# Hybrid decoder step: DeltaNet's z blocks 10 to 21 moved in halves into the attention's loop over pairs, with the convolution in pieces beside them

## The chip, the cores and the metric

One core of one Trainium2 chip runs the whole step in one launch. The metric is the device time in microseconds, the median of the runs shown. Engines: TensorE (PE) multiplies, its weight loads are shown apart (PEld), VectorE (DVE), ScalarE (ACT) and GpSimd (POOL) work elementwise, SyncE (SP) issues most of the DMAs. The engines run their own streams and meet at semaphores.

## What is computed

Two layers over N = 520 columns of width 1024: 512 prompt tokens and 8 single-token samples (T = 512, B = 8, HALF = 260). Per layer:

```python
x = x + 1/2 * SwiGLU_1(RMSNorm(x))
h = RMSNorm(x); z = h @ w_in
A: sparse attention (compressed / selected / window branches)
B: gated DeltaNet (short causal conv on q/k/v, delta rule in chunks)
C: HGRN2
x = x + merge(A, B, C) @ w_out
x = x + 1/2 * SwiGLU_2(RMSNorm(x))

def causal_conv(x_new, buf, w):        # before the delta rule
    xx = concatenate([buf, x_new], axis=1)
    return sum(xx[:, j:j + T] * w[j] for j in range(4))
```

With 512 tokens and 64-token blocks all blocks are selected, so the selected and the window branch are both plain causal attention over 512 rows with their own K and V.

## The kernel before

**Layout.** Everything stands transposed: 128 features on the partitions, 520 columns in the free dimension. z is made in 42 blocks of 128 columns of w_in (zi): 0 to 9 are the attention's q, k and v, 10 to 21 DeltaNet's q, k and v (four each), 22 to 25 its output gate, 26 to 41 HGRN2's; a small tile (gates, decays) comes after block 9. A product in f32 accuracy is made of three f16 products, w_hi by h_hi, w_hi by h_lo and w_lo by h_hi, so a block is 8 depths by 3 products by 2 halves of 260 columns, 48 matmuls (`products`, L2018 to L2030, called by `z_block`).

**Weights.** Each weight tile is fetched by SP (L2007, 512 KB) into one of two raw buffers, ScalarE makes w_hi (`split_hi`, L2012), GpSimd makes w_lo (`split_lo`, L2016); the ring has four tiles. SP may fetch tile n when tile n - 2 is split. SP goes through the tiles in order and has other DMAs in between: after z tile 16 the attention's new K and V are written back, after tile 17 DeltaNet's states are loaded (`D.load`, L816 and L817, behind `wait_left`: the attention is done), and after tile 43, the last of z, DeltaNet's outputs are written (`D.write_back`, L819 to L826, behind the step sa7). The first tiles of the merge (in_w_mg) are fetched only after that.

**The attention's loop over pairs** (`A.tensor`, `scalar`, `vector`, `pool`). For each of 4 query blocks t of 128 tokens there are 8 pairs (branch b, head column c), each of both KV groups g; 32 pairs i in all, and the scores of pair i have width w = 128 (t + 1). Per pair PE makes two score products in f32 (L349, K = 64), VectorE adds the distances and takes the minimum (L607), ScalarE exponentiates (L473), VectorE inverts the sums (L612), GpSimd scales (L513), PE transposes (L360), ScalarE and VectorE copy the two halves (L485, L623), and after four pairs PE makes the value products (L386). PE's stream runs scores(i), turn(i - 3), and values of the group before. The scores of a pair use banks 0 to 3 by turns, the transposes 4 and 5, the outputs 6 and 7. Each layer also has compressed scores turned (L368) and their values (L376).

**DeltaNet.** `for zi in range(10, 26)`: z_block, then `D.during_z`, which puts column sums of squares (`sums`, L894 and L895) after blocks 18 and 22 and the decay sums (gcl) after 24. ScalarE copies each block to cx (L1172 to L1174, or silu to dz, L1176), and for groups of four takes silu of the convolved rows (L1182) and squares (L1185). VectorE waits for a group of four blocks and then convolves, four taps by four rows of 512 columns (L1291, L1293). Then `D.tensor` runs the chunked delta rule, some 120 us in which PE waits for the chain of the other engines.

**Blocks 26 to 41** run with DeltaNet's end in between (`D.during_next`): after 26 small sums, after 27 and 28 the products with the 32 sample states (16 each, L1105), after 29 and 30 the norm sums (L1143, L1148), after 32 to 35 a spread (L1114), after 36 to 39 two outer products each (L1121). `vector_states` adds each to the states and gives sa0 to sa7 (L1496, L1500). HGRN2's own stage starts with sa7. A block zi waits until block zi - 2 has been copied, and ScalarE's copy of a block stands behind its split for the block before.

## Time and profile before

| | us |
|---|---|
| runs of the kernel before | 3437.97, 3439.61, 3445.85 (median 3439.61) |
| profiled execution, its own time | 3443.68 |
| its span, first to last instruction | 3441.9 |
| PE busy | 3154.1 (92%) |
| VectorE, ScalarE, GpSimd busy | 1078.4, 1082.3, 1129.9 |
| mean granted clock of TensorE | 0.926 of full speed |

The profiled execution took 1.8 us more than its span and lies 4.1 us above the median of the runs. PE's busy time contains waits inside its pipeline, so it is an upper bound of its work. The trace gives start and duration of each instruction, what ended the idle time before it, and for any stretch the busy time of each engine and the clock granted to TensorE (1.00 is 2.4 GHz, 0.50 is 1.2 GHz).

### The profile page before, as it was taken

Reading aid. Unit: us, or ns where it says so; the run is one execution under the profiler, and the core shown is the slowest. Engines: PE = TensorE matmul, PEld = TensorE weight load, DVE = VectorE, ACT = ScalarE, POOL = GpSimd, SP = SyncE. Lnnn points to the kernel's source line nnn. Section 1 sums busy time; section 2 is a strip of 40 time slices with the busy share of each in tenths; the row PEclk is TensorE's granted clock in tenths of the full one; section 3 lists DMA queues with packets and bytes.
Section 4 is the critical chain, followed back from the end, with each engine's and each line's share of the span. In section 5 each row is a group of like instructions: output and inputs, shape, how many; then the busy total and the mean of one; then the engine's idle time right before and its main releaser. Section 6 shows DMA issues by size and latency. Waiting matters only on the chain.

```text
span 3441.9 us, 69990 instructions
## 1 busy us (share of the span) xinstructions
PE 3154.1 (92%) x29292; PEld 2717.5 (79%) x29292; DVE 1078.4 (31%) x1981; ACT 1082.3 (31%) x1846; POOL 1129.9 (33%) x664
## 2 busy tenths in 40 slices
PE   6999898897888998999989998978978889989999
PEld 5888796387777887888878887864877788878887
DVE  3221202454244335221232212033542444352212
ACT  3332222432222323333233323224412223233322
POOL 3443320333121343443434443113331213334434
PEclk9999995998897999999999999959988979989999
DMA  4343320030021332332323433200200303323333
GB/s 142 114 149 89 115 88 1 1 106 20 26 96 40 93 120 80 98 98 87 104 90 117 138 95 119 67 1 33 87 8 28 125 27 93 120 74 98 98 92 116
DMA packets 87637, 283.27 MB, mean 82 GB/s; under 512 B 13330, under 2 KB 26514, under 8 KB 84882
## 3 DMA queue, kind: packets, MB, share of 16 engines
q1 hardware_dynamic: 87298, 278.54, 26.2%
q8 instruction: 155, 2.54, 0.3%
q10 hardware_dynamic: 144, 1.86, 0.2%
q14 instruction: 40, 0.33, 0.0%
HBM read 265.28 MB, written 15.09 MB: 81 GB/s over the span
## 4 chain that ended last, share of the span: by engine, by line
issue 53%; PE 21%; POOL 19%; DVE 3%; ACT 1%; POOLq 1%; DMA 1%; DVEq 0%; ACTq 0%; SPq 0%
POOL w_lo L2016 18%; PE pair L2026 8%; PE pair L249 2%; PE pair L386 1%; PE pair L349 1%; PE pair L360 1%; PE pair L335 1%; PE pair L298 1%; PE pair L103 1%; ACT arena L473 1%; PE pair L660 1%; PE pair L984 1%; PE pair L986 0%; PE pair L894 0%; PE pair L974 0%
## 5 line engine op out<-in xcount | busy, mean ns | idle before, releaser
L2016 POOL TENSOR_TENSOR w_lo<-raw,w_hi 128x1024 f16<-128x1024 f32 x452 | 995.4, 2213 | 1864.0 <-ACT w_hi L2012 1864.0
L2026 PE MATMUL pair<-h_hi,w_hi 128*128 128x260 f16 x2752 | 771.6, 280 | 35.3 <-DVE h_lo L2443 18.1
L2026 PE MATMUL pair<-h_lo,w_hi 128*128 128x260 f16 x2752 | 768.1, 279 | 0.0
L2026 PE MATMUL pair<-h_hi,w_lo 128*128 128x260 f16 x2752 | 767.8, 279 | 0.0
L2035 PE MATMUL pair<-arena,w_hi 128*128 128x260 f16 x4096 | 694.8, 277 | 28.2 <-DVE arena L2453 16.4
L2012 ACT ACTIVATE w_hi<-raw 128x1024 f16<-128x1024 f32 x452 | 464.5, 1052 | 568.2 <-PE pair L2035 389.6
L2035 PE MATMUL pair<-h_hi,w_hi 128*128 128x260 f16 x2176 | 599.6, 276 | 1.4 <-ACT mixed L1726 1.4
L2035 PE MATMUL pair<-h_lo,w_hi 128*128 128x260 f16 x2176 | 599.5, 276 | 0.0
L2035 PE MATMUL pair<-h_hi,w_lo 128*128 128x260 f16 x2176 | 599.4, 275 | 0.0
L2035 PE MATMUL pair<-arena,w_lo 128*128 128x260 f16 x2048 | 566.3, 276 | 0.0
L2035 PEld LDWEIGHTS pair<-arena,w_hi 128*128 128x128 f16 x4096 | 402.7, 99 | 88.2 <-POOL w_lo L2016 26.5
L2026 PEld LDWEIGHTS pair<-h_hi,w_hi 128*128 128x128 f16 x2752 | 275.0, 100 | 83.7 <-issue 33.8
L2026 PEld LDWEIGHTS pair<-h_hi,w_lo 128*128 128x128 f16 x2752 | 272.8, 99 | 44.4
L2026 PEld LDWEIGHTS pair<-h_lo,w_hi 128*128 128x128 f16 x2752 | 275.3, 100 | 41.1
L2035 PEld LDWEIGHTS pair<-h_hi,w_hi 128*128 128x128 f16 x2176 | 214.7, 99 | 31.1 <-ACT mixed L1726 1.8
L2035 PEld LDWEIGHTS pair<-h_hi,w_lo 128*128 128x128 f16 x2176 | 214.0, 98 | 29.7
L2035 PEld LDWEIGHTS pair<-h_lo,w_hi 128*128 128x128 f16 x2176 | 214.0, 98 | 29.3
L2322 ACT ACTIVATE arena<-pair 128x260 f32<-128x260 f32 x176 | 67.3, 382 | 512.8 <-PE pair L2035 259.4
L2450 DVE TENSOR_TENSOR arena<-arena,pair 128x260 f32<-128x260 f32 x176 | 74.4, 423 | 488.3 <-ACT arena L2322 488.3
L2035 PEld LDWEIGHTS pair<-arena,w_lo 128*128 128x128 f16 x2048 | 202.1, 99 | 28.9
L2453 DVE TENSOR_TENSOR arena<-arena 128x260 f32 x176 | 132.5, 753 | 234.1 <-ACT arena L2328 234.1
L513 POOL TENSOR_SCALAR arena<-arena,gate 128x128 f32<-128x128 f32 (+3 forms) x128 | 76.5, 607 | 321.3 <-DVE arena L612 321.3
(389 smaller groups left out, 3228.3 us busy)
## 6 DMA issues: line engine op xcount, KB each, us to landing
raw<-in_w_up SPq DMA_DIRECT2D x180, 512.0 KB, 3.7
raw<-in_w_z SPq DMA_DIRECT2D x84, 512.0 KB, 3.6
raw<-in_w_dn SPq DMA_DIRECT2D x64, 512.0 KB, 3.5
raw<-in_w_mg SPq DMA_DIRECT2D x48, 512.0 KB, 3.6
raw<-in_w_dn SPq DMA_DIRECT2D x32, 384.0 KB, 3.1
raw<-in_w_wb SPq DMA_DIRECT2D x24, 512.0 KB, 3.6
raw<-in_w_out SPq DMA_DIRECT2D x16, 512.0 KB, 3.6
arena<-in_slc_pages SPq DMA_DIRECT2D x32, 128.0 KB, 3.1
```

Source lines behind the costliest of these rows:

```text
L103: mm = pe.matmul(pair[w * g:w * g + w, a, c0 - a * HALF:c1 - a * HALF], f, ident[:, c0 - SUMS[j]:c1 - SUMS[j]], start=True, stop=True)
L249: mm = pe.matmul(pair[2 + k][:, g, 0:n], w1[k][o, r, :], cmpT[o, k, r:r + 16 * (n - 1) + 1:16], start=(r == 0), stop=(r == 31))
L298: mm = pe.matmul(bank(0)[:, 64 * k + 8 * s:64 * k + 8 * s + 8], kk, qm[:, 8 * s:8 * s + 8], start=True, stop=True)
L335: mm = pe.matmul(bank(3)[:, 8 * s:8 * s + 8], vv, spt[:, 192 * b + 64 * k + 8 * s:192 * b + 64 * k + 8 * s + 8], start=False, stop=(b == 1 ...
L513: e.tensor_scalar(pbuf[:, z, p, 0:w], pbuf[:, z, p, 0:w], fac[:, 2 * i + g:2 * i + g + 1], gate_tile(gate, t)[:, 8 + 8 * b + p:9 + 8 * b + ...
L2012: e.activation(w_hi[s % 4], raw[s % 2], ACT.Copy).then_inc(w_hi_done, 1)
L2016: e.tensor_tensor(w_lo[s % 4], raw[s % 2], w_hi[s % 4], ALU.subtract).then_inc(w_split, 1)
L2026: mm = pe.matmul(out, w[s % 4][:, k, :], xx[:, k, a * HALF:(a + 1) * HALF], start=(k == 0 and p == 0), stop=(k == KD - 1 and p == 2))
L2035: mm = pe.matmul(out, w[s % 4][:, kw, :], xx(kx), start=(first and i == 0 and p == 0), stop=(last and i == len(ks) - 1 and p == 2))
L2322: act_e.activation(sg[:, q, :], pair[q][:, 0, 0:HALF], ACT.Silu).then_inc(silu_done, 1)
L2450: dve.tensor_tensor(sg[:, q, :], sg[:, q, :], pair[q][:, 1, 0:HALF], ALU.mult).then_inc(gu_free, 1)
L2453: dve.tensor_tensor(act_lo[:, c, cols], sg[:, q:q + 1, :], act_hi[:, c, cols], ALU.subtract).then_inc(act_done, 1)
```

## The change

Blocks 10 to 21 leave the loop after the attention. `z_half` makes one half of a block (24 matmuls) in each of the first 24 iterations of the loop over pairs: four depths before the transposes, four after the value products. The first halves go to bank 6, the second to bank 7. To free these banks the scores use banks 0 to 2 by turns of one unit (was: two pairs of banks), the transposes 3 and 4, and all outputs bank 5. Probabilities sit in a ring of six pairs, value products come after every two pairs (256 columns each) and not after four. ScalarE copies each half and makes w_hi after every second, GpSimd makes w_lo after every second pair. VectorE convolves in 24 pieces of two operations with a drain, one after the scores of each of the iterations 9 to 32. The buffers of the convolution and some others have new places (cx in `mixed`, xs in the unused constant scanmask, cy at 18000).

After the attention ScalarE takes silu and square of groups 0 and 1, then blocks 22 to 25 run; the sums of squares stand behind 22 and 23, the decay sums behind 25. In blocks 26 to 41 the norm sums come after 27, all 32 state products after 29, and everything later one block later than it was, so the outer products stand after 37 to 40. SP loads the convolution's rows after tile 16, once the sample attention is done, and DeltaNet's sample states after tile 33, once the delta rule has ended (step s.3). In HGRN2 two buffers swap places.

```diff
@@ attention_plan
+RING = 6
-    pbuf = part(6736, 2 * 8 * 512).rearrange("p (s h n) -> p s h n", s=2, h=8)
-    ptb = part(14928, 2 * 4 * 8 * P).rearrange("p (s k g c n) -> p s k g c n", s=2, k=4, g=2, c=4)
+    pbuf = part(6736, RING * 2 * 512).rearrange("p (s g n) -> p s g n", s=RING, g=2)
+    ptb = part(12880, 2 * 4 * 4 * P).rearrange("p (s k g c n) -> p s k g c n", s=2, k=4, g=2, c=2)
+    def z_of(step):
+        return 10 + step // 2, step % 2
...
             def scores(i):
-                if i >= 2:
-                    pe.wait_ge(biased, 2 * (PAIRS * l + i - 1))
                 for g in range(2):
+                    a = 2 * i + g
+                    if a >= 3:
+                        pe.wait_ge(biased, 2 * PAIRS * l + a - 2)
-                    mm = pe.matmul(bank(2 * (i % 2) + g)[:, 0:w], ...
+                    mm = pe.matmul(bank(a % 3)[:, 0:w], ...
...
             for i in range(PAIRS + 5):
                 if i < PAIRS:
                     scores(i)
+                if i < 24:
+                    m["z_half"](pe, l, *z_of(i), 0, 4)
                 at = i - 3
                 if 0 <= at < PAIRS:
                     if at % 8 == 0:
                         cmp_turn(at // 8)
                     turn(at)
-                if at >= 4 and at % 4 == 0:
-                    if at % 8 == 4:
-                        cmp_values(at // 8)
-                    values(at // 4 - 1)
+                if at >= 3 and at % 2:
+                    j = (at - 3) // 2
+                    if j % 4 == 0:
+                        cmp_values(j // 4)
+                    values(j)
+                if i < 24:
+                    m["z_half"](pe, l, *z_of(i), 4, KD)
...  (ScalarE, after the copy of the transposes and before and after exp)
+                if 1 <= i < 25:
+                    m["D"].scalar_half(e, l, *z_of(i - 1))
                 if i < PAIRS:
                     exp(i)
+                if 1 <= i < 25 and z_of(i - 1)[1]:
+                    tile = m["z_tile"](z_of(i - 1)[0])
+                    m["split_hi"](e, l * TILES + tile, tile)
...  (GpSimd, after the scaling of pair i)
+                if i < 24 and z_of(i)[1]:
+                    tile = m["z_tile"](z_of(i)[0])
+                    m["split_lo"](e, l * TILES + 4 + tile, tile)
...  (VectorE, after the scores of pair i)
+                if 9 <= i < 33:
+                    m["D"].vector_conv(e, l, (i - 9) // 8, (i - 9) % 8)
@@ delta_plan
         def load(self, e, l):
-            m["A"].wait_left(e, l)
+            m["A"].wait_samples(e, l)
             e.dma_start(cin, m["ins"]["conv_in"][l]).then_inc(conv_in, 16)
+        def load_states(self, e, l):
+            e.wait_ge(V_.sem, V_.at("s.3", l))
             e.dma_start(ss, ...).then_inc(states_in, 16)
...  (during_z)
-            if zi == 18:
+            if zi == 22:
                 sums(0)
-            elif zi == 22:
+            elif zi == 23:
                 sums(1)
-            elif zi == 24:
+            elif zi == 25:
...  (during_next)
             elif zi == 27:
-                pe.wait_ge(states_in, 16 * (l + 1))
-                states(0)
-            elif zi == 28:
-                states(16).then_inc(*T_.step("sk"))
-            elif zi == 29:
                 w(S_, "oq")
...
+            elif zi == 29:
+                pe.wait_ge(states_in, 16 * (l + 1))
+                states(0)
+                states(16).then_inc(*T_.step("sk"))
-            elif zi == 30:
+            elif zi == 31:
...
-            elif 32 <= zi < 36:
-                spread_block(zi - 32)
-            elif 36 <= zi < 40:
-                outer(2 * (zi - 36))
-                outer(2 * (zi - 36) + 1)
+            elif 33 <= zi < 37:
+                spread_block(zi - 33)
+            elif 37 <= zi < 41:
+                outer(2 * (zi - 37))
+                outer(2 * (zi - 37) + 1)
...
+            for g in range(2):
+                silu(g)
+                e.drain()
+                e.activation(sq4[g], cy[:, 4 * g:4 * g + 4, :], ACT.Square).then_inc(*S_.step(f"lq{g}"))
-            for zi in range(10, 26):
+            for zi in range(22, 26):
...
+        def vector_conv(self, e, l, g, u):
+            j = u // 2
+            if u == 0:
+                e.wait_ge(m["z_used"], ZT * l + 10 + 4 * g + 4)
...
+            for i in range(2 * (u % 2), 2 * (u % 2) + 2):
+                c = 4 * g + i
+                if j == 0:
+                    e.tensor_scalar(cy[:, c, 0:T], cx[g][:, i, 0:T], cw[:, c, 0:1], None, ALU.mult)
+                else:
+                    e.scalar_tensor_tensor(cy[:, c, 0:T], cx[g][:, i, j:j + T], cw[:, c, j:j + 1], cy[:, c, 0:T],
+                                           ALU.mult, ALU.add)
+            e.drain() if u < 7 else e.drain().then_inc(*V_.step(f"conv{g}"))
@@ hybrid_step_kernel
+        def z_half(pe, l, zi, a, k0, k1):
+            if k0 == 0:
+                if a == 0:
+                    pe.wait_ge(w_split, l * TILES + z_tile(zi) + 3)
+                    pe.wait_ge(zh_used, 12 * l + zi - 10)
+                else:
+                    pe.wait_ge(z_used, ZT * l + zi)
+            for k in range(k0, k1):
+                for p, (w, xx) in enumerate(((w_hi, h_hi), (w_hi, h_lo), (w_lo, h_hi))):
+                    mm = pe.matmul(bank(6 + a)[:, 0:HALF], ...)
+            if k1 == KD:
+                mm.then_inc(z_ready if a else zh_ready, 1)
...  (SP, behind the fetch of z tile s)
                     if s == 16:
                         A.write_back(sp, l)
-                    if s == 17:
                         D.load(sp, l)
+                    if s == 33:
+                        D.load_states(sp, l)
                     if s == 43:
                         D.write_back(sp, l)
...  (PE)
-                for zi in range(10, 26):
+                for zi in range(22, 26):
                     z_block(l, zi)
                     D.during_z(pe, l, zi)
```

## Rows read from the trace of the kernel before

**Rows 1.** The page: the span of the one core
```profile
span 3441.9 us, 69990 instructions
```

**Rows 2.** Windows: stretch, us, busy of PE, PEld, DVE, ACT, POOL, clock, DMA
```profile
581.10:606.30 25.20, 22.85 (x88) 11.51 (x88) 10.86 (x68) 13.45 (x58) 9.16 (x20) 0.50 0.00 1
606.30:643.80 37.50, 29.47 (x158) 13.47 (x158) 19.20 (x76) 19.92 (x64) 15.66 (x26) 0.98 0.00 1
643.80:686.40 42.60, 35.11 (x172) 16.15 (x170) 18.66 (x53) 18.46 (x45) 13.42 (x18) 0.92 0.00 1
686.40:782.90 96.50, 96.50 (x843) 84.66 (x841) 48.77 (x81) 40.75 (x69) 33.37 (x15) 0.96 0.33 102
2289.90:2393.60 103.70, 83.79 (x416) 39.41 (x416) 48.68 (x196) 51.53 (x167) 38.24 (x64) 0.88 0.00 1
2393.60:2491.70 98.10, 98.10 (x842) 85.64 (x841) 48.82 (x81) 40.75 (x69) 33.35 (x15) 0.95 0.31 100
```

**Rows 3.** Windows: first 3.3 us of the dense z blocks, same columns
```profile
406.30:409.60 3.30, 3.29 (x15) 1.89 (x16) 3.23 (x5) 1.27 (x2) 0.00 (x0) 0.50 0.00 0
```

**Rows 4.** Waits of PE, pairs 8 to 23: total, times, longest
```profile
PE pair L360 <- POOL arena L513: 4.1, 3, 1.5
```

**Rows 5.** Timeline (start us, us), ScalarE: z blocks 20 and 21 copied
```profile
747.01 0.39 ACT L1172 ACTIVATE arena<-pair 128x260 f32<-128x260 f32 x1 [10.69 <-PE pair L2026]
752.35 0.39 ACT L1172 ACTIVATE arena<-pair 128x260 f32<-128x260 f32 x1 [3.67 <-PE pair L2026]
```

**Rows 6.** Timeline, PE: value products of groups 6 and 7
```profile
672.36 5.35 PE L386 MATMUL pair<-arena 128*64 128x512 f32 x16
682.84 3.65 PE L386 MATMUL pair<-arena 128*64 128x512 f32 x16 [0.87 <-DVE arena L623]
```

**Rows 7.** Timeline, VectorE: copy, reciprocal and one score of a pair of width 512
```profile
668.27 0.69 DVE L623 COPY arena<-pair 128x512 f32<-128x512 f32 x1
668.87 0.16 DVE L612 RECIPROCAL arena<-arena 128x2 f32<-128x2 f32 x1
669.48 0.69 DVE L607 CUSTOM_DVE_ANT_0 arena<-pair,const 128x512 f32<-128x512 f32 x1 [0.46 <-PE pair L349]
```

**Rows 8.** Timeline, VectorE: eight of the last group's convolution steps
```profile
762.33 7.26 DVE L1293 SCALAR_TENSOR_TENSOR arena<-arena,vec 128x512 f32<-128x512 f32 x8
```

**Rows 9.** Timeline, GpSimd: pair scaling, weight split, VectorE beside it
```profile
669.23 1.51 POOL L513 TENSOR_SCALAR arena<-arena,gate 128x512 f32<-128x512 f32 x2 [1.04 <-DVE arena L612]
...
961.27 2.12 POOL L2016 TENSOR_TENSOR w_lo<-raw,w_hi 128x1024 f16<-128x1024 f32 x1 [2.80 <-ACT w_hi L2012]
...
961.36 2.58 DVE L1485 TENSOR_TENSOR mixed<-mixed,arena 128x512 f32<-128x512 f32 x1
...
989.01 0.69 DVE L1500 TENSOR_TENSOR arena<-arena 128x512 f32<-128x512 f32 x1
```

**Rows 10.** Timeline: outer product, write-back, ScalarE split; window of idle PE
```profile
1005.71 1.95 PE L1121 MATMUL pair<-const,arena 128*128 128x128 f32 x16
...
1009.72 0.35 SPq L823 DMA_DIRECT2D out_conv_p<-arena  x1
...
1019.95 1.06 ACT L2012 ACTIVATE w_hi<-raw 128x1024 f16<-128x1024 f32 x1 [20.56 <-DMA raw<-in_w_mg]
...
1013.00:1021.60 8.60, 0.00 (x0) 0.03 (x1) 0.00 (x0) 1.65 (x3) 0.51 (x1) 0.75 0.83 305
```

**Rows 11.** Timeline, PE: half of the state products; and the window around it
```profile
917.18 3.63 PE L1105 MATMUL pair<-arena 128*128 128x2 f32 x32
...
916.00:927.00 11.00, 11.00 (x87) 9.42 (x85) 0.00 (x0) 2.04 (x3) 2.12 (x1) 0.84 0.21 69
```

**Rows 12.** Timeline, ScalarE: the silu of a group of four, and a table load
```profile
753.89 1.95 ACT L1182 ACTIVATE arena<-arena 128x2080 f32<-128x2080 f32 x1
773.63 1.28 ACT L1188 ACT_TABLE_LOAD   x1
```

**Rows 13.** DMA issues from 640 to 1000 us: KB each, us to landing
```profile
arena<-in_dn_in SPq DMA_DIRECT2D x1, 2048.0 KB, 8.1
```

More of the change, by code:

```diff
@@ L704, in delta_plan @@
     idc = levc[:, 6, :]
-    cx = part(0, 12 * 515, 12)
-    xs = part(6180, 12 * B * 4).rearrange("p (c b j) -> p c b j", c=12, b=B)
-    cy = part(6564, 12 * N, 12)
+    cx = [blocks_of(m["mixed"][:, 4 * N * i:4 * N * i + 4 * 515], 4) for i in (1, 2, 1)]
+    xs = m["free"][:, 0:384].rearrange("p (c b j) -> p c b j", c=12, b=B)
+    cy = part(18000, 12 * N, 12)
     def four(at):
@@ new lines, in silu @@
+            def silu(g):
+                w(V_, f"conv{g}")
+                e.activation(cy[:, 4 * g:4 * g + 4, :], cy[:, 4 * g:4 * g + 4, :], ACT.Silu).then_inc(*S_.step(f"silu{g}"))
+            for g in range(2):
[3 more added lines that the diff above has]
+            for zi in range(22, 26):
+                e.wait_ge(m["z_ready"], ZT * l + zi + 1)
+                e.activation(halves(dz[:, zi - 22, :]), both(zi % 2), ACT.Silu).then_inc(m["z_used"], 1)
+                m["split_hi"](e, l * TILES + m["z_tile"](zi), m["z_tile"](zi))
+                if zi == 22:
+                    silu(2)
+                elif zi == 23:
+                    w(V_, "ga")
+                    e.activation(ga, ga, ACT.Exp, scale=-1.0)
+                    e.activation(ea, vec_of("alog"), ACT.Exp).then_inc(*S_.step("ge"))
+                    e.drain()
+                    e.activation(gl, ga, ACT.Ln, bias=ones[:, 0:1]).then_inc(*S_.step("gl"))
@@ L1258, in scalar_next, with vector_pads @@
                              ACT.Square).then_inc(*S_.step("oqs"))
-            elif zi == 31:
+            elif zi == 32:
                 w(V_, "ov")
                 e.activation(v48, v48, ACT.Sqrt, bias=m["eps"][:, :], scale=1.0 / P).then_inc(*S_.step("ostd"))
+        def vector_pads(self, e, l):
+            for x in cx[:2]:
+                a = e.memset(x[:, :, 0:3], 0.0)
+            a.then_inc(*V_.step("pad"))
+        def vector_conv(self, e, l, g, u):
+            cw = vec_of("conv").rearrange("p (c j) -> p c j", j=4)
+            j = u // 2
+            if u == 0:
+                if g == 0:
+                    e.wait_ge(conv_in, 16 * (l + 1))
+                    e.tensor_copy(xs[:, :, :, 0:3], cin.rearrange("p (c b j) -> p c b j", c=12, b=B))
+                    e.drain()
+                e.wait_ge(m["z_used"], ZT * l + 10 + 4 * g + 4)
+                e.tensor_copy(cp.rearrange("p (c j) -> p c j", c=12)[:, 4 * g:4 * g + 4, :], cx[g][:, :, T:T + 3])
+                e.tensor_tensor(xw, xs[:, 4 * g:4 * g + 4], cw[:, 4 * g:4 * g + 4, :].unsqueeze(2)
+                                .to_broadcast([P, 4, B, 4]), ALU.mult)
+            if u == 2:
+                e.tensor_reduce(cy[:, 4 * g:4 * g + 4, T:N], xw, AX_X, ALU.add)
+            for i in range(2 * (u % 2), 2 * (u % 2) + 2):
[6 more added lines that the diff above has]
+            e.drain() if u < 7 else e.drain().then_inc(*V_.step(f"conv{g}"))
         def vector(self, e, l):
```

206 lines of the change are left out of this document (89 added, 117 removed), and 2 rows, old and new, of the table V_.

## The prediction, made before the change was run

> **What bounds the kernel now.** I read the page first: one core, a span of 3441.9 us [rows 1]. Then the windows of the stretches that the change touches, with PE's busy time and clock side by side [rows 2]. Layer 0's loop over pairs takes 105.3 us (581.1 to 686.4), layer 1's 103.7. In it PE is idle 2.35 + 8.0 + 7.5 = 17.9 us, and pairs 0 to 7 run at half clock throughout: 22.85 us of work that at full clock would be 11.4. Blocks 10 to 25 behind it take 96.5 us with PE busy in all of it: PE's work alone bounds them. So two stretches stand one behind the other, of which the first leaves PE time and clock unused and the second lacks only PE. A z block costs 5.34 us: that is how far apart ScalarE's first copies of blocks 20 and 21 start [rows 5]. The waits say why PE idles in the pairs: it waits for GpSimd's scaling, the end of a chain through four engines [rows 4]; no engine is full there (VectorE 48.7 of 105 us, ScalarE 51.8, GpSimd 38.2, the sums of the first three lines of [rows 2]).
>
> The last view is the end of the z blocks [rows 10], since the change moves the outer products there. SP issues the write-back at 1009.7, 2.1 us after the last outer product has ended; merge tiles are fetched behind it, ScalarE's split of the first one ends a wait of 20.6 us, and PE is idle for 8.6 us before block 41, because block 39's copy stands behind that split.
>
> **The change part by part, per layer.**
>
> (a) Blocks 10 to 21 leave their stretch: 12 x 5.34 = 64.1 us less. What is left of it is 32.4.
>
> (b) Pairs 0 to 23 now hold PE's own work plus these 64.1 us. The work: 11.4 (pairs 0 to 7 at full clock) + 29.5 (pairs 8 to 23, clock 0.98) = 40.9. Does the filling cover the waits? One iteration is now 64.1/24 = 2.67 us of z and some 1.7 of attention. VectorE needs in the widest of these pairs less than in a pair of width 512, which I work out under (c) as 3.4; ScalarE has 51.8/32 = 1.6 us on average and takes a copy and half a split more; GpSimd has some 1.3 and half of 2.12. All stay below an iteration, and transposes run three iterations behind the scores, so waits of up to 1.5 us [rows 4] vanish. I take no idle time. Weights: one tile per 8 to 10 us is wanted, ring and raw buffers are four and two tiles deep, nothing waits. The clock: where dense z blocks follow a half-clock stretch, the first 3.3 us run at 0.50 and what follows at full clock [rows 3]; so 1.7 us are lost at the start. For 48 changes between z and attention I add 1 us; the bounds are 0 and 5 (0.1 us for each). Sum: 40.9 + 64.1 + 1.7 + 1.0 = 107.7, against 62.7 now: +45.0.
>
> (c) Pairs 24 to 31 and the tail have no z, but VectorE gets the last convolution group. Now they take 42.6 us, 35.1 of them busy. Per pair of width 512 VectorE has two scores, a copy and a reciprocal: 3 x 0.6 + 0.15 = 1.95 us by the distance of their starts [rows 7]. The convolution: 7.26 us for eight steps is 0.91 each [rows 8]; if one of them met a weight split (below, 1.9 us), the others took 0.67. Two steps and a drain: 1.4 to 1.9. So VectorE needs 3.4 to 3.9 us per pair, PE's share is (35.1 - 8.8)/8 = 3.3 and the present pace 33.8/8 = 4.2, where 8.8 is the tail, from the end of group 6's value products (672.4 + 5.3 = 677.7 [rows 6]) to 686.4. I take 3.7 and 8.4 for the tail, whose value products are now halved: 38, against 42.6: -4.6. Lower bound: 31.7, PE's work without the 3.4 us that its clock of 0.92 costs (the value products of group 6 took 5.35 where the same sixteen later took 3.65 [rows 6]). Upper bound 49, under the rivals.
>
> (d) The outer products stand one block later. They end one block (5.3 us) later, and with them sa7, the write-back, SP's fetch of the merge tiles behind it, ScalarE's split, block 39's copy and block 41. Block 40 no longer fills the time behind the last outer product; PE's idle stretch grows from 8.6 to about 14 us. +5.3. This is a part of the change that costs what nothing hides. Bounds: 0, if something in the chain had slack (I see none), and 7.
>
> (e) States: two groups of sixteen cost some 5.3 us each: 3.6 of their own and 1.7 because the clock falls to half in the block behind, for a mean of 0.84 in 11 us is 3.5 us at half [rows 11]. As one group the second half would itself run at lower clock. I take +1.0; bounds -1.7 (one fall fewer) and +5 (all at half). They are now loaded at s.3 and not in the attention; 2 MB land in 8.1 us [rows 13], three blocks and the norm sums, over 20 us, pass before they are used. SP queues the fetch of tile 34 behind that DMA; it is wanted some 30 us later. 0.
>
> (f) After the attention ScalarE does a copy (0.6), a table load, a silu and a square, 0.6 + 1.28 + 2 x 1.95 = 5.8 us [rows 12], before `sums(0)` behind block 22 (5.34): +0.7 with semaphores. Sums(1) and the decay sums come a block later each and find their inputs: gate exponentials, logarithm and roots need some 10 us on ScalarE, sums and clock make these four blocks 32 us long. The decay sums behind 25 instead of 24 lose the block that covered them, but ScalarE reaches its exponential of them only after copy and split of block 25, so DeltaNet's chain starts when it did. 0. Two memsets on VectorE before the loop: +0.2. The DMA of the convolution's rows and the constants: 0.
>
> **Sum per layer:** -64.1 + 45.0 - 4.6 + 5.3 + 1.0 + 0.7 + 0.2 = -16.5 us; both layers -33. The profiled execution took 3443.7: 3410.7. It lies 4.1 above the median of the runs, so the median comes to **3407 us**. Differences up to 0.2% (7 us) can't be told from no change.
>
> **A rule against it.** A VectorE operation with two SBUF inputs that met GpSimd's weight split took 2.58 us, and it ended 0.55 us after the split; the same operation alone takes 0.69 [rows 9]. Convolution steps are of that kind, and in the pairs they now stand beside both the splits and the scaling (1.51 us per pair). By the Trainium skill (GPSIMD Engine Reference, Specifications) GpSimd's SBUF interfaces are shared with VectorE, with contention for instructions in a 2-port mode or with two SBUF inputs. The trace agrees for the split; beside the scaling no such operation stands, since the pair's VectorE work reads PSUM.
>
> **The rivals.**
>
> 1. *The port costs a little.* In pairs 24 to 32 a step finds the scaling in its way for one 0.76 us piece or two: 9 x 0.76 to 1.5 = 7 to 11 us, giving the upper 49 of (c). Up to pair 23 iterations have 1 us and more to spare. Gain 5.5 to 9.5 per layer: about 3424.
>
> 2. *The port decides (slower).* Were each convolution step held for a whole 1.9 us, VectorE would need 3.4 + 3.8 = 7.2 us per pair: nine late pairs lose 3.5 each, and fifteen earlier ones about 1.7, together 56 per layer, 40 net, so 3520 us. It turns the sign once the pairs lose 16.5 us, 1.8 per late pair. Against it: there GpSimd has only pieces of 0.76 us, and the first step comes 1.2 us after the reciprocal that releases them.
>
> 3. *The clock stays at half in pairs 0 to 7.* For 25 us of attention work at 0.50 it did not rise [rows 2], though PE was 90% busy. With z inside, 11.4 + 21.4 us would double: +31 per layer, slower, 3469. Against it: z is three quarters of each such iteration and alone raised the clock in 3.3 us [rows 3].
>
> 4. *It gains more.* (c) at PE's bound, (e) and (d) smaller: 26 per layer, 3388.
>
> 5. *It doesn't overlap:* if an unseen wait keeps z from filling the idle time, the clock's 11.4 - 1.7 us less (d), (e) and (f), 7.2, remain: gain 2.5 per layer, 3435.
>
> **How the numbers follow.** Forecast 0.72, rivals 1 to 5: 0.10, 0.03, 0.03, 0.08, 0.04. The range takes the forecast's own bounds (b high 4, c 4, e 4 per layer, not all at once: 3394 to 3420), rival 1 and most of 4: 3390 to 3426. Faster by over 0.2%: 0.72 + 0.10 + 0.08 = 0.90; within it, rival 5: 0.04; slower, rivals 2 and 3: 0.06.
>
> **What would show it.** Loop over pairs: about 146 us, with clock near 1.00 from its fourth microsecond and no PE waits over 1 us before pair 24; VectorE's waits for PE gone in pairs 25 to 32. Blocks 22 to 25: 32 to 33 us. Block 41 behind an idle stretch of 14 us. State products one group of 64 in 7 to 11 us. Wrong would be: iterations of more than 4.7 us before pair 24, convolution steps over 1.5 us beside the scaling, a clock of 0.50 after pair 2, or DeltaNet's stage longer than before.

## The result, and the profile after

| | before | changed |
|---|---|---|
| median of 10 runs, us | 3443.60 | 3430.66 |
| lowest to highest | 3437.97 to 3448.33 | 3423.03 to 3435.24 |
| profiled execution: its own time, span | 3443.68, 3441.9 | 3434.73, 3432.9 |
| mean granted clock | 0.926 | 0.926 |

The changed kernel's ratio to the one before is **0.9966**, 95% interval 0.9957 to 0.9974: faster by 0.34%, about 13 us. The forecast was 3407 with a range from 3390 to 3426. The sign was right and the size was not: 33 us were promised (from 3439.6 to 3407), and 13 came.

First the windows of the changed kernel, layer by layer: from the small products to the first pair, pairs 0 to 23, pairs 24 to 31 with the tail, blocks 22 to 25. The columns are those of [rows 2]: busy of PE, PEld, DVE, ACT, POOL, then the clock and the DMA's share and rate.

```profile
464.20:587.60 123.40, 108.04 (x830) 101.38 (x827) 19.12 (x46) 21.43 (x45) 6.34 (x3) 0.67 0.09 32
587.60:697.50 109.90, 107.72 (x848) 77.38 (x848) 50.32 (x180) 54.81 (x167) 46.58 (x55) 0.98 0.18 54
697.50:742.20 44.70, 35.60 (x228) 19.42 (x228) 32.79 (x75) 19.95 (x48) 17.91 (x21) 0.96 0.04 13
742.20:775.40 33.20, 32.68 (x265) 28.16 (x265) 4.11 (x20) 22.30 (x23) 6.39 (x3) 0.90 0.14 36
...
2287.60:2397.40 109.80, 107.64 (x847) 77.33 (x847) 50.74 (x180) 54.83 (x167) 46.58 (x55) 0.98 0.18 54
2397.40:2442.20 44.80, 35.70 (x229) 19.58 (x229) 32.81 (x75) 20.00 (x49) 17.92 (x21) 0.96 0.04 13
2442.20:2475.30 33.10, 32.57 (x264) 28.20 (x263) 4.10 (x20) 22.24 (x23) 6.39 (x3) 0.90 0.13 36
```

From the first pair to the end of block 25 it was 201.8 us [rows 2: 581.1 to 782.9]; it is now 109.9 + 44.7 + 33.2 = 187.8, 14.0 less where the working had 22.8 less. The filling did what it should: in pairs 0 to 23 PE is busy in 107.7 of 109.9 us at clock 0.98, against 0.50 for the first eight pairs before. The third line holds the loss: PE is idle for 9.1 of 44.7 us there, VectorE busy for 32.8, where [rows 2] have 18.7.

PE's waits in those two stretches (total, times, longest), up to pair 23 and behind it:

```profile
PE pair L355 <- DVE arena L615: 9.8, 1, 9.8
PE pair L366 <- ACT arena L489: 1.1, 3, 0.5
PE pair L366 <- DVE arena L634: 1.0, 3, 0.4
```

```profile
PE pair L366 <- issue: 6.6, 7, 2.0
PE pair L366 <- ACT arena L489: 2.1, 1, 2.1
PE pair L366 <- DVE arena L634: 0.2, 1, 0.2
```

L366 is the transpose (L360 before). The waits for GpSimd's scaling [rows 4] are gone. The 9.8 us of the first fence lie before the loop. What is left up to pair 23 are 1.1 + 1.0 us for the copies of the compressed probabilities (L489, L634). Such waits stood in the kernel before too (1.0 us before L360 in pairs 8 to 23); the working had put them at nothing. Behind pair 23 there are nine waits of up to 2.1 us; for seven of them the profile names no releaser ("issue").

Then the end of the z blocks, which answers to [rows 10] and [rows 11]:

```profile
925.45 9.64 PE L1128 MATMUL pair<-arena 128*128 128x2 f32 x64
...
1009.20 0.35 SPq L846 DMA_DIRECT2D out_conv_p<-arena  x1
1009.58 0.43 SPq L847 DMA_DIRECT2D out_conv_s<-arena  x1
1010.06 0.43 SPq L848 DMA_DIRECT2D out_dn_p<-arena  x1
1010.53 0.46 SPq L849 DMA_DIRECT2D out_dn_s<-arena  x1
1011.03 0.45 SPq L2047 DMA_DIRECT2D raw<-in_w_mg  x1
...
1019.48 1.06 ACT L2052 ACTIVATE w_hi<-raw 128x1024 f16<-128x1024 f32 x1 [27.74 <-DMA raw<-in_w_mg]
1020.45 0.59 ACT L1736 ACTIVATE arena<-pair 128x520 f32<-128x520 f32 x1
...
1021.13 0.38 PE L2066 MATMUL pair<-h_hi,w_hi 128*128 128x260 f16 x1 [14.00 <-issue]
```

The chain is there as written: write-back, fetch behind it on SyncE's queue, ScalarE's split, the copy (L1736) that stood behind the split, block 41 after 14.00 us of idle PE, 5.4 more than the 8.6 before. From the first product for the samples behind block 26 to HGRN's first transposes it takes 128.2 us in both layers; before it took 121.9 and 122.4.

The first line of the windows is code that was not changed, and took 123.4 us; before it took 117.0 and 118.8. That, 11 us over both layers, is as much as the whole result, so the first question was whether it belongs to the change.

### The profile page after: what moved, and what is told of

Same layout as the page of the kernel before. It is cut to its first block, busy times and chain, and to the rows that moved or that the text cites. A ratio compares the mean times of both kernels' runs of the same rounds, so it can differ in the third digit from the quotient of the medians.

```text
span 3432.9 us, 70214 instructions
## 1 busy us (share of the span) xinstructions
PE 3152.3 (92%) x29452; PEld 2729.0 (79%) x29452; DVE 1057.7 (31%) x1987; ACT 1091.1 (32%) x1848; POOL 1128.3 (33%) x664
## 4 chain that ended last, share of the span: by engine, by line
issue 54%; PE 22%; POOL 19%; DVE 3%; ACT 1%; POOLq 1%; DMA 1%; DVEq 0%; ACTq 0%; SPq 0%
POOL w_lo L2056 18%; PE pair L2066 4%; PE pair L2102 4%; PE pair L254 2%; PE pair L355 1%; PE pair L392 1%; PE pair L366 1%; PE pair L303 1%; PE pair L340 1%; PE pair L106 1%; PE pair L680 1%; PE pair L1007 1%; PE pair L1009 0%; PE pair L917 0%; DVE arena L1416 0%
## 5 line engine op out<-in xcount | busy, mean ns | idle before, releaser
L2066 PE MATMUL pair<-h_hi,w_hi 128*128 128x260 f16 x2368 | 664.8, 281 | 44.9 <-issue 28.0
L2066 PE MATMUL pair<-h_lo,w_hi 128*128 128x260 f16 x2368 | 662.1, 280 | 0.0
L2066 PE MATMUL pair<-h_hi,w_lo 128*128 128x260 f16 x2368 | 662.0, 280 | 0.0
L2075 PE MATMUL pair<-h_hi,w_hi 128*128 128x260 f16 x2176 | 599.4, 275 | 1.4 <-ACT mixed L1764 1.4
L2075 PE MATMUL pair<-h_lo,w_hi 128*128 128x260 f16 x2176 | 599.3, 275 | 0.0
L2075 PE MATMUL pair<-h_hi,w_lo 128*128 128x260 f16 x2176 | 599.2, 275 | 0.0
L2066 PEld LDWEIGHTS pair<-h_hi,w_hi 128*128 128x128 f16 x2368 | 237.1, 100 | 86.9 <-issue 43.5
L2066 PEld LDWEIGHTS pair<-h_hi,w_lo 128*128 128x128 f16 x2368 | 235.2, 99 | 38.4
L2066 PEld LDWEIGHTS pair<-h_lo,w_hi 128*128 128x128 f16 x2368 | 237.1, 100 | 35.6
L2075 PEld LDWEIGHTS pair<-h_hi,w_hi 128*128 128x128 f16 x2176 | 214.6, 99 | 31.0 <-ACT mixed L1764 1.8
L2075 PEld LDWEIGHTS pair<-h_hi,w_lo 128*128 128x128 f16 x2176 | 213.8, 98 | 29.6
L2075 PEld LDWEIGHTS pair<-h_lo,w_hi 128*128 128x128 f16 x2176 | 213.9, 98 | 29.3
```

What stands on the lines that cost most here:

```text
L2066: mm = pe.matmul(out, w[s % 4][:, k, :], xx[:, k, a * HALF:(a + 1) * HALF], start=(k == 0 and p == 0), stop=(k == KD - 1 and p == 2))
L2075: mm = pe.matmul(out, w[s % 4][:, kw, :], xx(kx), start=(first and i == 0 and p == 0), stop=(last and i == len(ks) - 1 and p == 2))
```

## The experiments

Thirteen other kernels were run, and the two under study once more. Times of different groups of runs are compared through their ratios to the kernel before, which was run beside each group. "Loop end" is pairs 24 to 31 with the tail.

| run | median us | ratio | 95% interval |
|---|---|---|---|
| changed kernel | 3430.66 | 0.9966 | 0.9957 to 0.9974 |
| no_conv2 | 3428.89 | 0.9961 | 0.9948 to 0.9974 |
| z_after_loop | 3458.33 | 1.0047 | 1.0030 to 1.0064 |
| outer_back | 3423.27 | 0.9941 | 0.9924 to 0.9958 |
| fetch_first | 3404.76 | 0.9886 | 0.9867 to 0.9904 |
| before_fetch_first | 3419.44 | 0.9932 | 0.9918 to 0.9946 |
| conv2_late | 3420.67 | 0.9939 | 0.9928 to 0.9951 |
| no_split | 3427.56 | 0.9958 | 0.9945 to 0.9971 |
| z_spread | 3435.95 | 0.9979 | 0.9968 to 0.9991 |
| fetch_outer | 3399.68 | 0.9879 | 0.9864 to 0.9893 |
| spread_fetch | 3405.16 | 0.9892 | 0.9878 to 0.9906 |
| conv_first | 3427.82 | 0.9963 | 0.9949 to 0.9976 |
| conv_first_fetch_outer | 3403.11 | 0.9879 | 0.9864 to 0.9895 |
| all_three | 3389.46 | 0.9850 | 0.9835 to 0.9866 |

### Both kernels once more: is the stretch before the loop part of the change?

before_again and after_again are the two kernels unchanged, one profiled execution each.

> The kernel before, unchanged, for another trace. Theory D (the stretch from the small products to the first pair, where nothing was changed, is long or short by where the clock's falls lie, at random): it takes 117 to 124 us per layer in this kernel too, and at least one of its two layers lies 3 us or more from the 117.0 and 118.8 of the first trace. Theory E (the changed kernel itself makes it 5 us longer): 117 to 119 in both layers.

> The changed kernel, unchanged, for another trace. Theory D: 117 to 124 us in that stretch, the two layers not alike or unlike the 123.4 and 123.5 of the first trace. Theory E: 123 to 124 in both. The loop over pairs again 110 us up to pair 24 and 44.8 behind it, blocks 22 to 25 again 33.

They took 3439.84 and 3433.35 us. The stretch from the small products to the first pair, first the kernel before and then the changed one:

```profile
463.80:582.50 118.70, 103.48 (x830) 96.58 (x828) 19.02 (x44) 21.43 (x45) 6.34 (x3) 0.72 0.09 31
2165.60:2289.00 123.40, 108.13 (x832) 101.70 (x829) 19.02 (x44) 21.43 (x45) 6.33 (x3) 0.67 0.09 30
```

```profile
463.70:587.20 123.50, 108.11 (x830) 101.29 (x829) 19.12 (x46) 21.44 (x45) 6.34 (x3) 0.67 0.09 32
2164.90:2282.20 117.30, 101.78 (x832) 95.13 (x830) 19.12 (x46) 21.44 (x45) 6.34 (x3) 0.73 0.10 33
```

The same instructions take 117 or 123 us in either kernel, with a mean clock of 0.73 or 0.67. Theory D holds: it is where the clock's falls lie in that execution, and no part of the change. A difference of two single profiles can therefore be off by 6 us per layer before any edit is looked at.

### The loop end: steps of the convolution, or the new banks?

no_conv2 (the convolution of v left out, zeros in its place):

```diff
-                if 9 <= i < 33:
-                    m["D"].vector_conv(e, l, (i - 9) // 8, (i - 9) % 8)
+                if 9 <= i < 33:
+                    if i < 25:
+                        m["D"].vector_conv(e, l, (i - 9) // 8, (i - 9) % 8)
```

> Leaves out the convolution of v (the last four of its twelve blocks): in pairs 25 to 32 VectorE has no steps, and zeros stand for that part. Theory A (VectorE's queue, its copies and scores behind the steps, holds pairs 24 to 31): that part with its tail falls from 44.7 us to 37 to 39 per layer, the kernel by 12 to 14 us, to about 3418. Theory B (the new banks and ring make these pairs slow, whatever VectorE has between them): it stays at 43 to 45 us, the kernel within 3 us of the changed one.

z_after_loop (new banks and ring; halves, their copies, splits and convolution behind the loop):

```diff
-                if i < 24:
-                    m["z_half"](pe, l, *z_of(i), 0, 4)
...
-                if i < 24:
-                    m["z_half"](pe, l, *z_of(i), 4, KD)
+            for i in range(24):
+                m["z_half"](pe, l, *z_of(i), 0, KD)
```

> The attention with its new score banks, single output bank and ring of six, but all of blocks 10 to 21, their copies, splits and convolution behind the loop. Theory A: the loop alone takes what it took before, 102 to 105 us, its last part 42 to 43. Theory B: the structure costs, pairs 24 to 31 with the tail take 44 to 46, the whole loop 107 or more. Either way the kernel is slower than the changed one, by some 17 to 25 us per layer (the filling is lost, and the convolution stands behind block 21): 3465 to 3480.

Windows of no_conv2, loop end and blocks 22 to 25 in layer 0, and the loop end in layer 1; then both parts of z_after_loop's loop in layer 0, and its loop end in layer 1:

```profile
692.60:732.40 39.80, 33.30 (x229) 18.98 (x229) 19.70 (x55) 20.04 (x49) 16.81 (x21) 1.00 0.05 14
732.40:768.70 36.30, 35.78 (x264) 30.88 (x263) 4.10 (x20) 22.17 (x23) 6.38 (x3) 0.81 0.11 32
2392.30:2432.40 40.10, 33.60 (x229) 19.19 (x229) 19.69 (x55) 20.00 (x49) 16.80 (x21) 1.00 0.05 14
```

```profile
587.50:647.10 59.60, 51.15 (x271) 27.02 (x271) 28.86 (x140) 32.66 (x117) 23.54 (x44) 0.82 0.00 1
647.10:687.70 40.60, 33.68 (x229) 19.36 (x229) 19.84 (x60) 20.39 (x51) 14.74 (x20) 1.00 0.01 1
...
2358.80:2401.00 42.20, 35.28 (x229) 20.23 (x229) 19.87 (x60) 20.32 (x51) 14.75 (x20) 0.96 0.00 1
```

Without the group the loop end falls from 44.7 and 44.8 to 39.8 and 40.1 us, 4.8 us per layer. Not all of that is the convolution's steps: the clock is 1.00 here and was 0.96 there, and z_after_loop, which has no steps in the loop, takes 40.6 us at 1.00 and 42.2 at 0.96. The next run parts the two. Theory B falls: with the new banks and nothing between the pairs the loop takes 100.2 us in layer 0 and 103.0 in layer 1, no more than the 105.3 and 103.7 of [rows 2]. But 40 is not the 37 to 39 of theory A, and not my 38. PE is idle for 6.5 us of it even with VectorE half empty. The copy of the compressed probabilities is 2.1 of these; the rest are five waits of up to 2.0 us before transposes, for which the profile names no releaser. By the kernel's semaphores they can be for the copies or the scaling of pairs before.

Nor did the kernel fall by 12: it fell by 0.05%, which is nothing that can be told. Blocks 22 to 25 took 36.3 us instead of 33.2, in both layers (36.4 in layer 1), with the clock at 0.81 instead of 0.90. The norm sums behind block 22, in the changed kernel and then in this one:

```profile
748.16 3.73 PE L917 MATMUL pair<-const,mixed 128*128 128x1 f32 x32 [0.52 <-ACT mixed L1188]
```

```profile
738.23 5.35 PE L922 MATMUL pair<-const,mixed 128*128 128x1 f32 x32 [0.52 <-ACT mixed L1193]
```

Same group, same wait, 3.73 or 5.35 us. In the changed kernel the clock fell behind this group, in no_conv2 within it:

```profile
750.00:751.90 1.90, 1.90 (x19) 1.90 (x20) 0.00 (x0) 1.89 (x2) 0.00 (x0) 1.00 0.00 0
```

```profile
740.20:743.50 3.30, 3.30 (x17) 3.30 (x17) 0.00 (x0) 3.30 (x4) 0.00 (x0) 0.50 0.00 0
```

So 3.1 of the 4.8 us went back to the clock one stage later. z_after_loop came out at 3458, not 3465 to 3480. From the first pair to the end of block 25 it took 201.2 and 204.1 us, hardly more than the 201.8 before: the convolution I had added is hidden there too. What makes it 16 us slower than the kernel before is the rest of the change: behind block 26 it took 128.2 us in both layers, 6 more than before.

### The last group behind the loop

```diff
-                if 9 <= i < 33:
+                if 9 <= i < 25:
                     m["D"].vector_conv(e, l, (i - 9) // 8, (i - 9) % 8)
+            for u in range(8):
+                m["D"].vector_conv(e, l, 2, u)
...
-                if zi == 22:
+                if zi == 24:
                     silu(2)
```

> On the changed kernel the last convolution group stands on VectorE behind the loop over pairs instead of between pairs 25 and 32, and its silu behind block 24. Theory A: pairs 24 to 31 with the tail take 40 us instead of 44.8, as without that group. What the run is for is what becomes of the 5 us: theory F (blocks 22 to 25 give 3 of them back, since the clock falls deeper behind their sums, as without the group): these blocks take 36 us instead of 33 and the kernel gains 1 to 4 us. Theory G (that was for want of the group's work on the engines): 33 us, and a gain of 9 to 10.

Loop end and blocks 22 to 25, layer 0 and layer 1:

```profile
691.60:733.10 41.50, 35.01 (x229) 19.90 (x229) 22.73 (x65) 20.19 (x49) 16.86 (x21) 0.96 0.05 14
733.10:769.40 36.30, 35.77 (x264) 30.97 (x262) 11.85 (x32) 22.18 (x23) 6.38 (x3) 0.81 0.12 34
2389.20:2430.60 41.40, 34.90 (x229) 19.94 (x229) 22.62 (x65) 20.06 (x49) 16.87 (x21) 0.96 0.05 14
2430.60:2463.60 33.00, 32.48 (x264) 28.04 (x262) 11.85 (x32) 22.16 (x23) 6.38 (x3) 0.90 0.14 36
```

Layer 0 gave 3.1 us back and layer 1 nothing, so neither F nor G holds in both. By the ratio, 0.9939 against 0.9966, some 9 us stay on the average, 3.3 per layer of them in the loop end. That is what the steps cost there: the clock is 0.96 as in the changed kernel, and the rest of no_conv2's 4.8 us, 1.5, is a fall of the clock that no_conv2 was spared.

### Place in the queue, or VectorE's time?

conv_first moves the call of `vector_conv` from behind the scores to between the copy and the reciprocal:

```diff
                     copy_pt(at)
+                if 9 <= i < 33:
+                    m["D"].vector_conv(e, l, (i - 9) // 8, (i - 9) % 8)
                 if 2 <= i < PAIRS + 2:
                     invert(i - 2)
...
-                if 9 <= i < 33:
-                    m["D"].vector_conv(e, l, (i - 9) // 8, (i - 9) % 8)
```

> On the changed kernel, VectorE's convolution steps of an iteration stand behind the copy of the transposed probabilities and ahead of the reciprocal and the scores, instead of behind the scores. Same work, other place in the queue. Theory I (the place costs: the copy that the next transposes wait for stands behind steps that nobody waits for): pairs 24 to 31 with the tail take 40 to 42.5 us instead of 44.8. Theory J (VectorE's time as such, or GpSimd's and VectorE's shared way to SBUF, costs, wherever the steps stand): 44 to 46. The kernel: 3422 to 3428 by I, 3429 to 3433 by J. The reciprocals and the scaling come later by 1.4 us in this order; if that link is the tight one, 46 or more.

```profile
690.90:734.50 43.60, 35.56 (x229) 20.42 (x229) 31.34 (x75) 20.05 (x49) 16.88 (x21) 0.96 0.05 17
2388.10:2432.90 44.80, 36.91 (x229) 20.89 (x229) 31.21 (x74) 20.03 (x49) 16.90 (x21) 0.92 0.05 17
```

43.6 and 44.8 us; the second had the clock at 0.92. In conv_first_fetch_outer it is 45.9 and 45.8 at 0.89. At the changed kernel's clock, 0.96, the new order took 1.1 us less (43.6 against 44.7, one layer), which lies between the two theories: I named 40 to 42.5, J 44 to 46. The ratio, 0.9963, can't be told from the changed kernel's, and the median, 3427.82, lies in I's range. So the place in the queue is worth some 1 us per layer, and most of the 3.3 us stay: wherever the steps stand, something of the next pair stands behind them.

What the shared way to SBUF had in it shows in rows of the changed kernel, at the one place in layer 0's loop end where a step met a weight split, with the copy that stands behind the steps and the transposes that wait for that copy:

```profile
703.84 2.74 DVE L1317 TENSOR_SCALAR arena<-mixed,vec 128x512 f32<-128x512 f32 x2
706.73 0.56 DVE L641 COPY arena<-pair 128x384 f32<-128x384 f32 x1
...
703.66 2.24 POOL L2056 TENSOR_TENSOR w_lo<-raw,w_hi 128x1024 f16<-128x1024 f32 x1
...
707.39 0.52 PE L366 MATMUL pair<-const,arena 128*128 128x128 f32 x3 [1.95 <-issue]
```

Two steps that take 0.48 us each alone took 2.74 together, ending 0.7 us after the split: 1.8 us lost. The loss is on PE's path: the transposes waited 1.95 us and started 0.1 us after the copy's end. That wait is not in no_conv2 or conv2_late; it makes up most of the 2.6 us by which PE is idle longer in the changed kernel's loop end (9.1 us) than in theirs (6.5). Layer 1 has the same rows (2.75 us, a wait of 1.95). So by the traces more than half of the 3.3 us of the steps came by this one split. No run has the steps without it, so the share is read and not tested.

The 36 steps of the other form in layer 0 took 0.75 us in the median and 1.03 at most, although 1.5 us of scaling stood in nearly every pair:

```profile
L1319 DVE SCALAR_TENSOR_TENSOR arena<-mixed,vec,arena x36: 731/746/1030, 633.8 to 734.1; 128x512 f32<-128x512 f32 x36
```

By the Trainium skill (SBUF — State Buffer, section "SBUF: two separate sides") the pair of ports that VectorE and GpSimd share is an exclusive lock for a whole instruction. The trace agrees at the split. Beside the scaling the steps seldom met one in progress; where they did (722.68 and 726.32 us), two took 1.61 and 1.69 instead of 1.41, and once (733.67) it was the scaling that took 1.77 us instead of 0.76.

### Filling spread over all pairs

```diff
+    def step_at(i):
+        return 3 * (i // 4) + i % 4 if 0 <= i < PAIRS and i % 4 < 3 else None
```

and half block `step_at(i)` in pair i, on every engine; conv2_late's edits are in it. The convolution moved too: group 1's steps, which stood in pairs 17 to 24, stand in pairs 22 to 29 here, so the loop end has most of a group's steps again, and one pair of them met a weight split (3.40 us).

> On conv2_late, the 24 half blocks stand in three of every four pairs, to pair 30, instead of in each of pairs 0 to 23; convolution group 0 from pair 11, group 1 from pair 22, group 2 behind the loop. Theory H (what is lost in pairs 24 to 31 is TensorE idle for want of filling: 44.8 us with 35.7 busy): the loop with its tail takes 145 to 148 us instead of 154.6, and the kernel 6 to 14 us less than the changed one, 3417 to 3425; the part against conv2_late, whose loop took 151.1 and 152.1, is 4 to 6 us per layer unless blocks 22 to 25 give it back. Rival (the unfilled pairs among the narrow ones idle as much as is saved behind, or the clock stays low longer): within 3 us of conv2_late's 3420.7 or slower.

The loop took 157.1 us in layer 0 and 157.6 in layer 1, against 152.1 and 151.1 of conv2_late; blocks 22 to 25 took 36.3. Theory H fell. Six halves are 16.0 us of work at full clock (6 x 2.67). Pairs 24 to 31 with six of them should take 41.4 + 16.0 = 57.4 us less what idle time they fill; they took 58.4 and 58.6. Pairs 0 to 23, with six fewer, took 98.7 and 99.0 instead of 110.6 or 109.7, where 94 were due. PE's two long waits behind pair 23:

```profile
PE pair L369 <- POOL arena L533: 3.0, 1, 3.0
PE pair L369 <- ACT arena L493: 2.1, 1, 2.1
```

So in the pairs without a half PE waits as long as before or longer (2.1 and 3.0 us, against 2.1 and 2.0 in conv2_late), and a half in the iteration beside it doesn't cover that. Dense filling of some pairs with none in the others was the better order here; how much of the difference is group 1's steps in the loop end is not shown. spread_fetch adds the edit of fetch_first (below) to it:

> z_spread with the edit of fetch_first, a version meant to beat both kernels. If the two add up as their places suggest, 24 to 26 us below z_spread's time; with z_spread at 3415, 3390. If HGRN's levels, which in fetch_first waited 3 to 4 us longer for VectorE, take more of it: 20 below.

Its ratio was 0.9892, some 30 us below z_spread's 0.9979: about the sum, and no better than fetch_first alone.

### The halves whole instead of split

```diff
-                    m["z_half"](pe, l, *z_of(i), 0, 4)
+                    m["z_half"](pe, l, *z_of(i), 0, KD)
```

and no second call behind the value products.

> On the changed kernel each half block of 24 products stands whole between the scores and the transposes of its pair, not 12 before them and 12 behind the value products. If the split matters (the transposes' copies then come later after the next scores, or the value products find their copies less ready), PE waits for the copies of probabilities grow from some 2 us per loop to 5 or more, and the kernel loses 3 to 10 us; if an iteration of 4.6 us covers every chain in either order, which my forecast assumed, it stays within 3 us of 3430.7.

0.9958 against 0.9966: within what can be told. Pairs 0 to 23 took 109.0 and 108.1 us instead of 109.9 and 109.8. The split around the transposes, the finest detail of the change, brings nothing.

### The outer products and SyncE's queue

outer_back puts sums, roots, spreads and outer products one block earlier again (the states in one group behind block 28):

```diff
-            elif 33 <= zi < 37:
-                spread_block(zi - 33)
-            elif 37 <= zi < 41:
+            elif 32 <= zi < 36:
+                spread_block(zi - 32)
+            elif 36 <= zi < 40:
```

> The outer products, the sums and roots of the samples back to where they stood before the change, all 64 state products in one group behind block 28. Theory C (the outer products one block later cost 5.3 us by way of the write-back, the fetch behind it and ScalarE's split): PE's idle time before block 41 falls from 14 to 8.6 us, the kernel by 9 to 11 us, to about 3420. Rival (the chain has slack, or the states' group in an earlier place gives it back): less than 3 us.

fetch_first moves the write-back on SyncE's queue behind four fetches:

```diff
-                    if s == 43:
-                        D.write_back(sp, l)
...
                     for s in range(12):
+                        if first and s == 4:
+                            D.write_back(sp, l)
```

> SyncE fetches the first four merge tiles before it waits for the end of the outer products and writes back. If theory C has the right link (SyncE's queue), the 14 us of idle TensorE before block 41 go to under 2, HGRN starts 12 to 14 us earlier in each layer, and the kernel falls by 24 to 28 us, to about 3405. Rival (the link is VectorE's last outer product itself, which HGRN awaits too, or the write-back then delays the fourth merge tile): the idle time moves behind block 41 or into the merge, and the kernel gains under 8 us.

before_fetch_first is that edit on the kernel before, fetch_outer both edits on the changed one:

> The kernel before with the one edit of fetch_first: SyncE fetches four merge tiles before the write-back. Theory C: the 8.6 us of idle TensorE before block 41 go, and with them 20 to 22 us in all, to about 3422; what the change under study brings beside this edit is then 17 to 20 us instead of 13, since its outer products a block later cost nothing any more. Rival (the idle stretch is the last outer product's, not the fetch's): under 8 us.

> fetch_first and outer_back together. Theory C: once SyncE's fetches no longer stand behind the write-back, the place of the outer products costs nothing, so that moving them back brings nothing, and the state products in their earlier place cost the 1.3 to 1.6 us of lower clock that outer_back showed: 3404 to 3409, against 3404.8 of fetch_first. Rival (a second link, VectorE's own work for the samples, that HGRN's levels wait for): 3396 to 3401.

PE's wait before block 41 in outer_back, its states, and SyncE's queue in fetch_first:

```profile
PE pair L2066 <- issue: 9.4, 1, 9.4
```

```profile
919.59 10.97 PE L1128 MATMUL pair<-arena 128*128 128x2 f32 x64
```

```profile
981.74 0.33 SPq L2047 DMA_DIRECT2D raw<-in_w_mg  x1
987.97 0.33 SPq L2047 DMA_DIRECT2D raw<-in_w_wb  x1
995.09 7.45 SPq L2047 DMA_DIRECT2D raw<-in_w_mg  x2
1011.32 0.35 SPq L846 DMA_DIRECT2D out_conv_p<-arena  x1
```

In outer_back the idle time fell by 4.6 us, not 5.3, and the group of states, a block earlier, took 10.97 us instead of 9.64. The stage from behind block 26 to HGRN took 125.0 and 124.6 us, against 128.2: 3.4 per layer, and some 9 us in all by the ratio: theory C, a little smaller for the lower clock under the states.

In fetch_first that stage took 111.9 us in both layers, 16.3 less, and the wait is gone; the median was 3404.76 where 3405 was forecast. It is the largest thing found here, and it was there before the change: before_fetch_first gained 0.68%, 23 us, twice as much as the change itself. The four fetches now go out between 981 and 1003 us, as soon as their buffers are free. Part of it comes back in HGRN, which starts earlier while VectorE is still at the samples' states: PE's waits in its levels that lead the list, first the changed kernel and then fetch_first, layer 0.

```profile
PE pair L1628 <- issue: 10.4, 5, 3.5
```

```profile
PE pair L1628 <- issue: 13.7, 5, 4.8
```

In fetch_outer this wait is 10.1 us again. Its ratio, 0.9879 against 0.9886, doesn't decide between theory C and the rival; if a second link by way of VectorE costs, it is little. Beside the edit the change brings 0.9886 / 0.9932 = 0.9954, some 16 us with an uncertainty of about 8, instead of 0.9966. That the outer products then cost nothing fits, but isn't shown by it. The stage itself says more: it takes 111.9 and 110.3 us in before_fetch_first and 111.9 twice in fetch_first, so of the 6.5 us that the change adds to it 0.8 are left. HGRN behind it takes 48.9 and 45.2 us in the one and 48.4 and 53.0 in the other, which is too unlike from layer to layer to say whether part of the cost moved there.

### The versions that beat both

> fetch_outer and conv2_late together, a version meant to beat both kernels. conv2_late was 10 us under the changed kernel, fetch_outer 31. If they add up: 3390; if the clock behind the sums of blocks 22 and 23 takes the late group's gain back in both layers: 3396 to 3400.

> fetch_outer and conv_first together. The sum of the two edits: 3399.7 less what conv_first brings, 3392 to 3398 by theory I, 3398 to 3402 by theory J.

all_three is outer_back, fetch_first and conv2_late together. **Ratio 0.9850 (0.9835 to 0.9866), median 3389.46 us**: 52 us below the kernel before, four times the change's gain, and the sum of its parts (3390). Blocks 22 to 25 took 33.1 us in both layers here, behind a loop end of 41.4:

```profile
735.00:768.10 33.10, 32.58 (x265) 28.10 (x263) 11.88 (x32) 22.25 (x23) 6.39 (x3) 0.90 0.14 38
...
2411.50:2444.60 33.10, 32.58 (x265) 28.27 (x263) 11.91 (x32) 22.25 (x23) 6.38 (x3) 0.90 0.13 38
```

Of the four layers with the last group late and the halves in pairs 0 to 23, three had 33 us and one 36. conv_first_fetch_outer has fetch_outer's ratio; its median, 3403.11, lies above what either theory named.

## Why the prediction was right in sign and wrong in size

The two traces of each kernel give four layers of each. Their means, in us per layer:

| stretch | before | changed | difference | forecast |
|---|---|---|---|---|
| small products to first pair | 119.5 | 121.9 | +2.4 (clock) | 0 |
| first pair to end of block 25 | 201.4 | 188.7 | -12.7 | -22.8 |
| DeltaNet's chunks | 127.8 | 126.8 | -1.0 | 0 |
| behind block 26 to HGRN | 122.0 | 128.5 | +6.5 | +6.3 |
| HGRN to the merge | 48.5 | 48.1 | -0.4 | 0 |

The sum, -5.2 per layer or 10 us in all, lies between the differences of the profiled spans (9.0 in the first pair of traces, 6.5 in the second) and the 13 us of the medians.

- **(a) and (f)**, blocks 22 to 25: 32.4 + 0.7 = 33.1 forecast; 33.2 and 33.1 measured, with the wait of 0.52 us for ScalarE that stood for the 0.7. Right. (In after_again 33.3 and 34.9, the second with the clock at 0.85.)
- **(b)**, pairs 0 to 23: 107.7 forecast, 109.9 measured; PE's busy time was 107.7. The clock rose and the waits for scaling went, as written. "I take no idle time" failed by 2.1 us: the copies of the compressed probabilities, a wait that the trace before shows too.
- **(c)**, pairs 24 to 31 with the tail: 38 forecast, 44.7 and 44.8 measured (in after_again 44.7, and 45.9 with the clock at 0.93). **This is the step that failed**, "so VectorE needs 3.4 to 3.9 us per pair [...] I take 3.7". Two steps did take 1.40 us where nothing held them. What was wrong was to take the need of the busiest engine as the pace. The pace was 4.2 before, at engines less than half full (PE apart), and nothing in the change loosened what it hangs on. The runs split the 6.7 us that are missing: 2 are a floor of 40 us at full clock (no_conv2; 40.6 in z_after_loop), 1.5 a fall of the clock within the stretch, which the sum had left out, and 3.3 the steps, though VectorE had room for their 11 us on average (conv2_late). Of these 3.3 the wait of 1.95 us behind the steps that the weight split held is the largest piece. That PE idles at the floor because copies, scores and transposes of neighbouring pairs wait for one another in turn is read from the waits and not shown by a run. The upper bound of 49, which I gave to the port alone, held. A slip beside it: "(35.1 - 8.8)/8 = 3.3" counts PE as busy in the whole tail, where it is idle for 1.5 us, so its share was 3.5.
- **(d)**: +5.3 and 14 us of idle PE forecast, 14.00 measured. **(e)**: +1.0 forecast, one group of 9.64 us. Together +6.3 against +6.5. Right, mechanism and size, and fetch_first shows that the link is the queue order and not the outer products.
- **Rivals 1 and 5** named the numbers on either side of the result, 3424 and 3435. Rival 1 was there in part: in each layer's loop end one pair of steps was held for 1.8 us and PE waited behind it, but by a weight split and not by the scaling, which it had priced. (Its "9 x 0.76 to 1.5 = 7 to 11" comes to 7 to 13.5.) Rival 5 was not: the filling did overlap. **Rivals 2 and 3** did not occur: of the two-input steps the slowest took 1.37 us (layer 1), and the clock in pairs 0 to 23 was 0.98. The range was too narrow because (c)'s upper bound had been given to one rival with a chance of 0.10, and because nothing in it allowed for single profiles that differ by 6 us per layer in stretches that nobody touched.

What stays open: what the last group of steps costs where it meets no weight split, why a fall of the clock behind the same sums is sometimes 3 us deeper, and whether fetch_outer beats fetch_first.

## What to carry to other kernels

Where an engine's queue waits for a neighbour in every iteration, its load says nothing about the pace: count added work as late, in part at least, even on an engine that is half idle (here 3.3 of 11 us), and look there for the one instruction that another engine holds: it can be half of the cost. Look at what stands *behind* a wait in a DMA queue before moving the work that ends the wait: reordering four fetches was worth 23 us by itself, where the large change gained 13. Compare at least two traces of each kernel before reading a few us out of a difference, and look first at stretches that were not edited.

## What was not expected of the hardware

The clock gives gains back and hands out others. The same 64 state products took 9.64 us in one place and 10.97 a block earlier; the same norm sums 3.73 or 5.35; the same stretch before the loop 117 or 123, blocks 22 to 25 33.1 or 36.3. In these traces PE's clock fell in or behind the norm sums and the state products, and how much work was caught in the fall differed from one execution to the next.

GpSimd's scaling, which stands beside the convolution in every pair, cost VectorE's steps almost nothing (0.75 us in the median beside it, 0.75 in the stage of z blocks before), while a single weight split cost 1.8 us, and PE a wait of 1.95.
